# Final row scaling of a MoE encoder block: three of eight chunks on ScalarE and GpSimd instead of VectorE

## What is computed

```python
def rms_norm(x, g):
    xf = x.astype(jnp.float32)
    y = xf * lax.rsqrt(jnp.mean(xf * xf, axis=-1, keepdims=True) + EPS)
    return (y * g.astype(jnp.float32)).astype(x.dtype)
...
        h = h + (routed + shared).reshape(bsz, s, d)
    return rms_norm(h, final_norm_g)
```

## Time and profile before

| | us |
|---|---|
| median of 3 runs | 1287.68 (1287.34 to 1287.98) |
| the profiled execution | 1288.58 |
| its span, first to last instruction | 1286.9 |
| busy in the span: PE / DVE / ACT / POOL | 1263.3 / 854.3 / 773.6 / 457.2 |
| granted clock of TensorE, share of full speed | 0.997 |

### The profile page before, as it was taken

How to read it: one execution, slowest core, us unless ns; L and a number is a source line. 1 busy time by engine, 2 the same in 40 slices (tenths; PEclk the granted TensorE clock), 3 DMA queues, 4 the chain that set the end, 5 groups by cost and what they waited for, 6 DMA issues and landing times.

```text
span 1286.9 us, 27300 instructions
## 1 busy us (share of the span) xinstructions
PE 1263.3 (98%) x6249; PEld 1051.8 (82%) x6250; DVE 854.3 (66%) x1222; ACT 773.6 (60%) x1087; POOL 457.2 (36%) x600
## 2 busy tenths in 40 slices
PE   8999989999999999999999999999999999999996
PEld 7888788888877888888888888888888888888885
DVE  5122563468956777767777687677677686777767
ACT  6222182232456777677777686677776776777763
POOL 1322140000023444444444444444444444444463
PEclk9999999999999999999999999999999999999998
DMA  9120352121468999999999999999999999999988
GB/s 336 33 70 1 139 219 99 66 94 46 168 230 305 318 336 331 304 317 331 327 329 315 329 333 330 339 326 335 339 330 302 326 356 298 342 316 327 342 246 249
DMA packets 81270, 337.21 MB, mean 262 GB/s; under 512 B 12753, under 2 KB 15953, under 8 KB 64593
## 3 DMA queue, kind: packets, MB, share of 16 engines
q1 hardware_dynamic: 53728, 250.73, 50.6%
q0 software_dynamic: 27360, 86.01, 27.5%
q10 hardware_dynamic: 144, 0.00, 0.0%
HBM read 288.14 MB, written 65.27 MB: 275 GB/s over the span
## 4 chain that ended last, share of the span: by engine, by line
PE 91%; DVE 3%; DMA 2%; ACT 2%; issue 1%; POOL 1%; SPq 0%; POOLq 0%; ACTq 0%; DVEq 0%
PE ps L856 38%; PE ps_out L870 19%; PE ps L523 9%; PE ps L505 7%; PE ps L660 6%; PE ps L717 4%; PE ps L878 1%; DMA yb_in<-y_rows_dram 1%; PE ps_out L699 1%; PE ps L608 1%; PE ps_out L745 1%; PE ps L745 1%; DMA w_in_sb<-in_w_in 1%; DMA y_rows_dram<-ob 1%; DVE ya_in L1795 1%
## 5 line engine op out<-in xcount | busy, mean ns | idle before, releaser
L856 PE MATMUL ps<-w_gu,xTh 128*128 x1488 | 467.7, 395 | 2.1 <-DVE xTl L1718 2.0
L1517 DVE TENSOR_TENSOR w_gu<-raw_gu,w_gu (+1 forms) x256 | 296.6, 1220 | 71.4 <-ACT w_gu L1181 71.4
L856 PEld LDWEIGHTS ps<-w_gu,xTh 128*128 128x128 f32 x1488 | 273.2, 188 | 56.5 <-issue 2.8
L856 PE MATMUL ps<-w_gu,xTl 128*128 x744 | 291.2, 391 | 0.0
L1181 ACT ACTIVATE w_gu<-raw_gu (+1 forms) x256 | 250.1, 1049 | 1.5 <-issue 1.5
L870 PE MATMUL ps_out<-w_dn,hTh 128*128 x744 | 241.2, 406 | 0.0
L1927 POOL DMA_INDIRECT y_rows_dram<-ob,idxs x90 | 146.3, 1625 | 141.6 <-ACT ob L1204 134.5
L1524 DVE TENSOR_TENSOR w_dn<-raw_dn,w_dn (+1 forms) x128 | 151.1, 1222 | 27.5 <-ACT w_dn L1185 25.7
L856 PEld LDWEIGHTS ps<-w_gu,xTl 128*128 128x128 f32 x744 | 139.7, 188 | 29.0
L870 PEld LDWEIGHTS ps_out<-w_dn,hTh 128*128 128x128 f32 x744 | 133.2, 189 | 25.9 <-issue 0.2
L870 PE MATMUL ps_out<-w_dn,hTl 128*128 x372 | 146.4, 394 | 0.0
(11 more groups left out here) (295 smaller groups left out, 1695.8 us busy)
## 6 DMA issues: line engine op xcount, KB each, us to landing
raw_gu<-in_w_gate SPq DMA_DIRECT2D x64, 1024.0 KB, 7.3
raw_gu<-in_w_up SPq DMA_DIRECT2D x64, 1024.0 KB, 11.5
raw_dn<-in_w_down SPq DMA_DIRECT2D x64, 1024.0 KB, 12.9
x_ring<-in_x SPq DMA_DIRECT2D x8, 512.0 KB, 3.6
w_in_sb<-in_w_in SPq DMA_DIRECT2D x8, 512.0 KB, 9.0
xh<-in_x SPq DMA_DIRECT2D x8, 512.0 KB, 8.1
w_out_sb<-in_w_out SPq DMA_DIRECT2D x1, 4096.0 KB, 21.9
hn_rows_dram<-rows SPq DMA_DIRECT2D x8, 512.0 KB, 2.6
```

The lines of the kernel that those rows point to most:

```text
L856: mm = pe.matmul(ps[3][:, :], x_[:, k, :], w_gu[:, bass.ds(at, 1), part, :, k, :], start=(k == 0 and part == 0 and x_ is xTh), stop=(k == ...
L1517: dv.tensor_tensor(gu_part(w_gu[:, :, 1, :, :, :], at, m), gu_part(raw_gu, at, m), gu_part(w_gu[:, :, 0, :, :, :], at, m).bitcast(F32), AL ...
```

## The change

The scales of chunks 0, 2 and 4 are no longer on DVE. For these chunks ACT multiplies `ya_in` by the root in place (`scaled(c)`, a Copy with a scale of one value for each partition), behind its square of chunk c+1. POOL then multiplies by `gf_row` in place, behind the root of chunk c+1. Two semaphores join them: `s_scaled` from ACT to POOL, `s_og` from POOL to SP's store. DVE skips these chunks.

```diff
+        s_scaled, s_og = sem("sums_scaled"), sem("out_rows_by_gpsimd")
...
             for c in range(NC):
-                sp.wait_ge(s_of, c + 1)
+                if c in BY_GPSIMD:
+                    sp.wait_ge(s_og, BY_GPSIMD.index(c) + 1)
+                else:
+                    sp.wait_ge(s_of, c + 1 - sum(g < c for g in BY_GPSIMD))
                 sp.dma_start(out_v[c], ya_in[:, c, :]).then_inc(s_ost, 16)
...
+            def scaled(c):
+
+                act.wait_ge(s_rf, c + 1)
+                act.activation(ya_in[:, c, :], ya_in[:, c, :], ACT.Copy, scale=rs[:, 4, c:c + 1]).then_inc(s_scaled, 1)
+
             for c in range(NC):
                 act.wait_ge(s_sum, c + 1)
                 act.wait_ge(s_sq2, NC) if c == 0 else act.wait_ge(s_sqf, c)
                 square(ya_in[:, c, :], D ** -0.5, 4, c, s_sqf)
+                if c - 1 in BY_GPSIMD:
+                    scaled(c - 1)
...
             for c in range(NC):
                 if c + 2 < NC:
                     add_last(c + 2)
+                if c in BY_GPSIMD:
+                    continue
...
+            gp.wait_ge(s_gf, 32)
             for c in range(NC):
                 rstd(4, c, s_sqf, s_rf)
+                if c - 1 in BY_GPSIMD:
+                    gp.wait_ge(s_scaled, BY_GPSIMD.index(c - 1) + 1)
+                    gp.tensor_tensor(ya_in[:, c - 1, :], ya_in[:, c - 1, :], gf_row[:, :], ALU.mult).then_inc(s_og, 1)
...
+BY_GPSIMD = (0, 2, 4)
```

## The result

| | before | after |
|---|---|---|
| median of 20 runs, us | 1287.44 | 1289.84 |
| the profiled execution, us | 1288.58 | 1289.83 |
| its span, us | 1286.9 | 1288.1 |
| busy from 1257.0 to the end, 30.0 and 31.1 us: DVE / ACT / POOL | 22.94 / 9.21 / 9.15 | 22.93 / 12.21 / 17.31 |

The ratio is 1.0019 (95% interval 1.0013 to 1.0025): 2.4 us slower, clear of noise. The point lies just inside the 0.2% that the prediction took as its bound, and the interval reaches to both sides of it. The windows row of the tail answers to the earlier trace rows: three scales have left DVE, and its busy time has not fallen.

The account below looks back on a forecast made before the run. It took PE's last matmul and the chain behind it as the floor, then POOL's in-order chain: rounds of 5.44, 5.44 and 4.49 plus the last root put chunk 7's scale +4.27 later, 1292.0 us; range 1288.8 to 1293.4.

Parts of the forecast that it names:

- the sum: POOL's chain in the tail, three rounds from 1268.36: scale of chunk 7 at 1285.82, +4.27 us; chance 0.70 including rival (c).
- the anchor: Start of POOL's chain, read from the trace of before: the root of chunk 1 ends at 1268.36.
- proof of the hold: POOL's L1845 at 1266.51 took 1.20 instead of 0.22, against DVE's scale of chunk 0 ending at 1267.63.
- idle by then: DVE, idle when chunk 1's root ends, starts that scale 0.04 later, POOL its next op 0.08 later; DVE goes first.
- rival (c): In the tail POOL takes the port first and DVE's scale waits; same time as the sum, chance inside its 0.70.
- the first meeting: POOL's multiplication of chunk 0 against DVE's scale of chunk 1 at the SBUF port; the multiplication stands until the scale is through.
- the signs that the prediction named: In the new profile: L2008 at 3.5 to 3.7 us, scale of chunk 7 near 1285.8, ACT's copies at 1.06.
- The best case of -1.4: Most the change could gain in the tail by taking three scales off DVE: -1.4 us, 0.11%.
- The 0.4: Gain if DVE's add of chunk 7 starts at 1276.70 instead of 1277.11, behind PE's last matmul.
- the 1.0: Gain if POOL's L1845 of chunk 7 no longer met DVE's scale of chunk 6, 1.20 instead of 0.22.
- (b): Only one or two of three POOL/DVE meetings happen: +2.3 to +3.3, 1290.0 to 1291.0; chance 0.11.
- (a): The port holds long instructions less, POOL's multiplications run from the start: +1.3, 1289.0, within 0.2%; chance 0.15.

Follow-up runs that it names:

- the kernel with the added wait: Changed kernel where POOL's multiplications of chunks 0, 2, 4 also wait for DVE's scales of 1, 3, 5: 1292.04 us, ratio 1.0037 to the kernel before.
- the kernel without the meetings: Changed kernel with DVE's scales of chunks 1, 3 and 5 left out, those rows stored unscaled: 1287.13 us against 1287.64 for the kernel before, ratio 0.9995.

## Why the prediction was right or wrong

**Slower, by POOL's chain: right.** The end is where POOL's roots let it be; the sum's path (multiplication, two roots, with DVE's scale in series, three times over) is the one in the chain of waits. From the moment POOL could first start its multiplication to the scale of chunk 7 the sum had 1268.44 to 1285.82, 17.38; the two traces of the changed kernel have 17.2.

**The size: wrong, 4.3 for 2.4.** The failed step is the anchor, "The root of chunk 1 ends at 1268.36". In the new trace it ends at 1265.44, and the multiplication starts at 1265.59, 2.85 earlier than 1268.44. In the trace of before, the anchor went back to this row:

```profile
1262.69 1.22 DVE L1785 TENSOR_TENSOR ya_in<-ya_in,yb_in 128x1024 f32<-128x1024 f32 x1 [1.39 <-DMA yb_in<-y_rows_dram]
```

The 2.85 has three parts.

- 0.90 is the change's own doing: from the second addition of `yb_in` to POOL's start it was 1268.44 - 1262.69 = 5.75 before and is 4.85 now, since the scale of chunk 0, which had held that root's L1845 for 1.0, is one of those moved. I had used that very row, 1.20 at 1266.51, as proof of the hold, and left its price in the sum.
- 1.43 is the load: the addition starts 13.96 ahead of PE's end before, 15.39 in the new trace. The trace of before had caught the latest one. The kernel before hides such a delay mostly behind PE (its distance rose from 4.55 to 4.90), so it hardly stood in its time, but it stood in full in my chain. I looked at the landing of `yv2` loads for chunks 2 to 7, and not at this one, though DVE's gap before it ended on it.
- 0.52 is the whole tail, which lies that much earlier in the new execution (PE's end 1276.13 against 1276.65), and says nothing of the change.

In distances this closes: 4.27 foreseen, less 0.90, less 1.43, less 0.17 of the chain behind the anchor, and 0.35 more since the kernel before is at 4.55 in its second trace and not at 4.90, is 2.12, the 6.67 - 4.55 of the traces.

**Who goes first: wrong, without consequence for a round.** I expected DVE first, "idle by then". With the earlier root, DVE was still at the addition of chunk 3, behind a wait for PE of 0.87, so POOL started first, all three times: rival (c). Its claim of the same time held per round: 5.48 against 5.44. For the first meeting the order counts, as the kernel with the added wait shows (2.0 us slower than the changed one). Of the signs that the prediction named, L2008 of 3.5 to 3.7 and ACT's copies of 1.06 are not there; scales of over 2 us on DVE, the sign of (c), are.

**The prices.** Multiplication 2.36 expected, 2.41 measured; L1858 behind a scale, 1.08; root 0.87 right. ACT's copy 1.06 expected, 1.15 measured, and it is not hidden: it stands on the chain in each later round, where POOL waits 0.3 for it. That the round came out at 5.44 for 5.48 is partly luck. Without a meeting the sum's terms make a round of 4.34, where the kernel without the meetings has 4.63, 0.3 more, mostly for that copy; the meeting adds 1.10 in the sum and measured 0.86 (1.08 instead of 0.22). The two errors cancel.

**The best case of -1.4: wrong in its size, without weight.** Leaving the three scales out gained nothing (ratio 0.9999). The 0.4 was the late load, and the 1.0 can't come back while the scale of chunk 6 reads two inputs in SBUF.

**Chances.** The likeliest case was given as over 0.2%. The ratio is 1.0019, so the kernel lies at that bound, on its inner side, which had 0.23. By its mechanism it is the forecast's case, in the form of (c); by its size, 1289.84, it is nearest to (b)'s lower end of 1290.0, though all three meetings took place. The stated range, 1288.8 to 1293.4, holds it only because it had been drawn down into (a), whose mechanism isn't what happened. The prediction's first paragraph also has the change behind the last matmul; the moved scales stand beside PE's last 10 us of matmuls, as its own next paragraph treats them.

## What to carry to other kernels

Work moved off an engine that another one already hides gains nothing: in the second trace of before DVE's last addition started 0.10 behind PE. Look then at what the receiving engine does for others, in order: POOL's roots release everything behind them. And before an anchor is taken from one trace, undo in it what the change undoes, and ask which load or wait sets it and whether the old path hid that.

## What the runs showed of the hardware

- A DVE scale with two inputs in SBUF that started after POOL's 128x1024 multiplication, also with two inputs in SBUF, ended 1.07 to 1.09 behind it, whenever it had started: it took 2.0 to 3.5 instead of 1.28. The other way round, a small POOL instruction of 0.22 that started after the scale ended some 0.08 behind it, and took up to 1.3. How a long POOL instruction fares that starts second beside a scale, no run here shows.
- With one tensor input, POOL's 128x1024 instruction (2.87) ran beside DVE's scale (1.27) without a loss to either, once it was running; a small one-input instruction that starts during the scale is held (0.39 in that run, 1.08 elsewhere). The prediction saw the first in L1972, and could not say which property of it mattered; that it is the one input, and not the kind of instruction, is likely but not shown.
- With the second input of DVE's scale in PSUM, POOL's small instruction took 0.22, and POOL's running multiplication did not hold DVE. The price is DVE's: instructions of 128x512 started 0.66 apart, and two took 1.40.
- ACT's in-place copy with a column as scale took 1.15 on 128x1024 fp32, against 1.06 for the copy without one of the earlier trace rows.
